# Mixture-of-experts blocks of 32 token slots instead of 64, with four column lanes side by side, in a two-layer backbone on one core

## The reference

```
u = modulate(h, sh2, sc2)
scores = sigmoid(u @ w_router); the best group of 4 experts, in it the best 2
hid = silu(x @ w_gate[e]) * (x @ w_up[e])       # 1024 -> 512, per expert e
y   = hid @ w_down[e]                           # 512 -> 1024
out = sum over the 2 chosen experts of y * score / (sum of the 2 scores)
h = layer_norm(DN_ALPHA * h + g2 * out, ln_g, ln_b)
```

## Time and profile before

| | |
|---|---|
| median of the runs | 1379.34 us |
| profiled execution: time, span | 1381.63 us, 1379.8 us |
| PE busy | 1174.8 us, 85% of the span |
| PE weight loads busy | 663.1 us, 48% |
| DVE, ACT, POOL busy | 543.6, 245.6, 192.9 us |
| mean granted TensorE clock | 0.923 of full |
| gate and up, lines 1307 and 1309, busy on their lanes | 352.0 and 352.6 us |
| down, line 1333 | 186.8 us |
| POOL copy 448, mean; gather 443, mean, median landing | 1.05; 1.12, 6.9 us |
| table loads of line 642 | 25, 1.28 us each |
| DMA traffic | 335.32 MB, mean 243 GB/s |

### The profile page before, as it was taken

One profiled execution on the slowest core, in us unless ns is written; L12 is line 12 of the kernel. 1 busy time (PEld: TensorE's weight loads), 2 busy tenths in 40 slices (PEclk: granted clock), 3 DMA queues, 4 the chain that ended last, 5 costly groups with the idle time before them and its releaser, 6 DMA issues.

```text
span 1379.8 us, 18949 instructions
## 1 busy us (share of the span) xinstructions
PE 1174.8 (85%) x6946; PEld 663.1 (48%) x6947; DVE 543.6 (39%) x1319; ACT 245.6 (18%) x606; POOL 192.9 (14%) x166
## 2 busy tenths in 40 slices
PE   3999799998985999999984399989679999999940
PEld 0444344454453565666542244444445666655620
DVE  0246543462555333333322703036543333333338
ACT  0222333341120111111112111021101111111110
POOL 0011100000001111111111332300021111111123
PEclk9899999998986999999987699999779999999975
DMA  9921399982242999739995782151549996689933
GB/s 326 382 77 61 137 355 352 360 320 100 83 182 69 362 381 374 268 94 368 383 380 178 232 292 89 61 213 46 198 136 382 378 375 213 228 285 373 373 119 135
DMA packets 142758, 335.32 MB, mean 243 GB/s; under 512 B 6872, under 2 KB 9344, under 8 KB 142592
## 3 DMA queue, kind: packets, MB, share of 16 engines
q1 hardware_dynamic: 122400, 286.88, 57.1%
q0 software_dynamic: 6624, 22.55, 5.5%
q10 hardware_dynamic: 13696, 25.38, 5.4%
HBM read 315.40 MB, written 27.79 MB: 249 GB/s over the span
## 4 chain that ended last, share of the span: by engine, by line
PE 75%; DVE 9%; SPq 6%; DMA 5%; issue 2%; ACT 1%; POOL 0%; ACTq 0%; DVEq 0%; PEldq 0%; POOLq 0%
PE PS L1307 13%; PE PS L1333 11%; PE PS L1309 9%; PE PS L1240 8%; PE PS L1391 8%; PE PS L1150 7%; SPq L302 4%; PE PS L1170 3%; PE PS L1086 3%; PE PS L1270 2%; PE PS L1181 2%; DMA ring<-in_e_up_dram 2%; PE PS L1317 2%; DMA RD<-expert_rows,yidx 2%; PE PS L1275 2%
## 5 line engine op out<-in xcount | busy, mean ns | idle before, releaser
L1307 PE MATMUL PS<-ring,RE 128*64 128x256 f32 x1120 | 257.1, 389 | 22.8 <-DVE RE L973 10.3
L1309 PE MATMUL PS<-ring,RE 128*64 128x256 f32 x1120 | 257.5, 390 | 0.0
L1307 PEld LDWEIGHTS PS<-ring,RE 128*64 128x64 f32 x1120 | 155.7, 141 | 81.6 <-issue 46.0
L1001 DVE TENSOR_TENSOR RE<-RE,PS 64x256 f32<-64x256 f32 x100 | 42.3, 423 | 352.9 <-ACT RE L647 352.9
L1309 PEld LDWEIGHTS PS<-ring,RE 128*64 128x64 f32 x1120 | 155.6, 141 | 28.5 <-issue 7.0
L1333 PE MATMUL PS<-ring,RE 128*64 128x512 f32 x560 | 136.2, 602 | 0.0
L1240 PE MATMUL PS<-ring,uT 128*128 128x512 f32 x256 | 111.2, 593 | 1.9 <-ACT G L611 1.1
L1391 PE MATMUL PS<-ring,uT 128*128 128x512 f32 x256 | 110.0, 592 | 0.0
L448 POOL COPY RFW<-RE 64x1024 f32<-64x1024 f32 x50 | 52.3, 1046 | 404.4 <-PE PS L1275 390.1
L1307 PE MATMUL PS<-uT,RE 128*64 128x256 f32 x416 | 94.9, 387 | 5.0 <-DMA RD<-in_e_up_dram 4.1
L1309 PE MATMUL PS<-RD,RE 128*64 128x256 f32 x416 | 95.1, 388 | 0.0
(11 more groups left out here) (214 smaller groups left out, 1482.4 us busy)
## 6 DMA issues: line engine op xcount, KB each, us to landing
ring<-in_w_ada_dram SPq DMA_DIRECT2D x24, 2048.0 KB, 12.0
ring<-in_e_gate_dram SPq DMA_DIRECT2D x22, 2048.0 KB, 16.3
ring<-in_e_up_dram SPq DMA_DIRECT2D x22, 2048.0 KB, 19.0
ring<-in_e_down_dram SPq DMA_DIRECT2D x22, 2048.0 KB, 20.0
RD<-in_e_up_dram SPq DMA_DIRECT2D x10, 2048.0 KB, 22.8
RFW<-in_e_down_dram SPq DMA_DIRECT2D x10, 2048.0 KB, 21.7
uT<-in_e_gate_dram SPq DMA_DIRECT2D x10, 2048.0 KB, 17.1
ring<-in_b_win_dram SPq DMA_DIRECT2D x4, 2048.0 KB, 8.3
```

The lines of the kernel that those rows point to most:

```text
L1001: V_.tensor_tensor(hid[:, 256 * h:256 * h + 256], gs[:, 256 * h:256 * h + 256], PS[BLK:P, h, 0:256], ALU.mult).then_inc(hid_rd[l][h], 1)
L1307: mm(PS[0:BLK, h, 0:256], xT[:, k, :], wg[:, k, 256 * h:256 * h + 256], start=(k == 0), stop=(k == DC - 1))
L1309: ins = mm(PS[BLK:P, h, 0:256], xT[:, k, :], wu[:, k, 256 * h:256 * h + 256], start=(k == 0), stop=(k == DC - 1))
```

## The change

`BLK` becomes 32, and `CG` = 128 / 32 = 4 is the number of column lanes. Gate and up each split in two halves of 256 columns, so that four matmuls of 256 columns (gate 0, gate 1, up 0, up 1) share one moment and one PSUM bank at partitions 0, 32, 64 and 96. Down splits the 1024 output columns in four lanes of 256. The silu and the product work on 64 partitions (both gate halves below each other) in two pieces of 128 columns, both behind the whole of gate and up, and one transpose of such a piece turns two hidden chunks at once. A block's output is 128 x 256 and goes out in four stores of 32 rows x 1 KB.

The row numbers of all blocks are made at once ahead of the loop: a slot number is split in its low five bits and the rest, and eight matmuls of two one-hot factors give a table `gidx` of 32 x 52. POOL has two gather buffers and copies the column that a gather reads to `gcol`. The Silu activation that makes the table load stands ahead of ACT's loop.

```diff
-BLK = 64
+BLK = 32
+CG = P // BLK
@@ row numbers, DVE
-                link(V_.tensor_copy(srel[:, :, :], slot[:, :, :]))
+                link(V_.tensor_scalar(sli[:, :, :], yidx[:, :, :], BLK - 1, None, ALU.bitwise_and))
+                link(V_.tensor_copy(slo[:, :, :], sli[:, :, :]))
+                link(V_.tensor_tensor(shi[:, :, :], slot[:, :, :], slo[:, :, :], ALU.subtract))
+                V_.tensor_tensor(ohlo, slo[:, :, :].rearrange("p k t -> p (k t)").unsqueeze(2).broadcast_to([P, 2 * NT, BLK]),
+                                 iota_s.unsqueeze(1).broadcast_to([P, 2 * NT, BLK]), ALU.is_equal)
+                for k in range(2):
+                    for j in range(NT):
+                        ins = V_.tensor_scalar(ohhi[:, NT * k + j, :], iota_b, shi[:, k, j:j + 1], tokid[:, j:j + 1],
+                                               ALU.is_equal, ALU.mult)
+                ins.then_inc(oh_rd[l], 1)
+                dve.wait_ge(ix_pe[l], 1)
+                V_.tensor_copy(gidx[:, :], PS[0:BLK, 6, 0:NCOL]).then_inc(ix_rd[l], 1)
@@ GpSimd, in the loop
-                        pool.wait_ge(xg_in[l], g * 16 + 16)
+                        pool.wait_ge(xg_in[l][1 - par], gg * 16 + 16)
+                        nc.gpsimd.tensor_copy(gcol[:, 1 - par:2 - par], gidx[:, bass.ds(g + 3, 1)]).then_inc(gc_used[l], 1)
                         pool.wait_ge(xt_pe[l], g + 1)
-                        hand_over()
-                        pool.wait_ge(ix_rd[l], g + 3)
+                        nc.gpsimd.tensor_copy(xg, xga[1 - par]).then_inc(xg_rd[l], 1)
...
-                        gather(par)
+                        gather(xga[1 - par], xg_in[l][1 - par], gcol[:, 1 - par:2 - par])
@@ ScalarE
+                A(warm[:, :], ones[:, 0:1], ACT.Silu)
                 with act.Fori(0, pairs) as gg:
-                    A(warm[:, :], ones[:, 0:1], ACT.Silu)
                     for par in range(2):
                         g = gg * 2 + par
+                        act.wait_ge(gu[l], g + 1)
                         for h in range(2):
-                            act.wait_ge(gu[l][h], g + 1)
-                            A(gs[:, 256 * h:256 * h + 256], PS[0:BLK, h, 0:256], ACT.Silu).then_inc(silu_rd[l][h], 1)
+                            A(gs[:, P * h:P * h + P], PS[0:2 * BLK, 0, P * h:P * h + P], ACT.Silu).then_inc(silu_rd[l][h], 1)
+                        for h in range(2):
                             act.wait_ge(ht_pe[l][h], g + 1)
-                            A(hidT[:, 2 * h:2 * h + 2, :], PS[:, 3 + h, 0:2 * BLK].rearrange("p (k s) -> p k s", k=2),
+                            A(hidT[:, h, :, :], PS[:, 3 + h, 0:2 * BLK].rearrange("p (h s) -> p h s", h=2),
                               ACT.Copy).then_inc(ht_rd[l][h], 1)
                         act.wait_ge(y_ev[l], g + 1)
-                        for q in range(2):
-                            act.dma_start(yscr[l][bass.ds(g * BLK, BLK), 512 * q:512 * q + 512],
+                        for q in range(CG):
+                            act.dma_start(yscr[l][bass.ds(g * BLK, BLK), 256 * q:256 * q + 256],
                                           ysb[par][BLK * q:BLK * q + BLK, :]).then_inc(y_st[l][par], 16)
@@ VectorE, in the loop: index(), onehot() and the wait for the gather go; the two products are
+                            V_.tensor_tensor(hid[:, P * h:P * h + P], gs[:, P * h:P * h + P],
+                                             PS[2 * BLK:P, 0, P * h:P * h + P], ALU.mult).then_inc(hid_rd[l][h], 1)
@@ TensorE, ahead of the loop
+                for n in range(2 * NT):
+                    ins = mm(PS[0:BLK, 6, 0:NCOL], ohlo[:, n, :], ohhi[:, n, :], start=(n == 0), stop=(n == 2 * NT - 1))
@@ TensorE, in the loop
+                        for k in range(DC):
+                            for q in range(CG):
+                                w, h = (wg, wu)[q // 2], q % 2
+                                ins = mm(PS[BLK * q:BLK * q + BLK, 0, 0:256], xT[:, k, :], w[:, k, 256 * h:256 * h + 256],
                                          start=(k == 0), stop=(k == DC - 1))
+                        ins.then_inc(gu[l], 1)
                         pe.wait_ge(xg_rd[l], g + 1)
                         turn_x()
+                        for h in range(2):
+                            pe.wait_ge(hid_rd[l][h], g + 1)
+                            nc.tensor.transpose(PS[:, 3 + h, 0:2 * BLK], hid[:, P * h:P * h + P],
+                                                ident[0:2 * BLK, 0:2 * BLK]).then_inc(ht_pe[l][h], 1)
                         landed(2)
+                        for h in range(2):
                             pe.wait_ge(ht_rd[l][h], g + 1)
+                            for k in (h, h + 2):
+                                for q in range(CG):
+                                    ins = mm(PS[BLK * q:BLK * q + BLK, 5, 0:256], hidT[:, h, k // 2, :],
+                                             wd[:, k, 256 * q:256 * q + 256], start=(k == 0), stop=(k == FC - 1))
+                        ins.then_inc(dn_pe[l], 1)
```

More of the change, by code:

```diff
@@ L51, in backbone @@
     NTHR = TOK // BLK - 1
+    NCOL = MAXB + 4
     SH1, SC1, G1, SH2, SC2, G2 = range(0, 6 * DC, DC)
@@ L161, in backbone @@
         slot = sb("slot", [P, 2, NT])
-        srel = sb("srel", [P, 2, NT])
+        slo = sb("slo", [P, 2, NT])
+        shi = sb("shi", [P, 2, NT])
+        sli = sb("sli", [P, 2, NT], I32)
         yidx = sb("yidx", [P, 2, NT], I32)
         table = [sb(f"table{l}", [1, NE + 3], I32) for l in range(DEPTH)]
-        gidx = sb("gidx", [P, 2], I32)
+        gidx = sb("gidx", [BLK, NCOL], I32)
+        gcol = sb("gcol", [BLK, 2], I32)
         at = {}
-        for name, width in (("slot", BLK), ("dec16", NE), ("dec4", NG), ("token", NT), ("thr", NTHR), ("pair", MAXB // 2)):
+        for name, width in (("slot", BLK), ("dec16", NE), ("dec4", NG), ("token", NT), ("thr", NTHR), ("pair", MAXB // 2),
+                            ("block", NCOL)):
             first = sum(b - a for a, b in at.values())
             at[name] = (first, first + width)
-        ic = sb("ic", [P, first + width], I32)
+        ic = RE[:, 512:512 + first + width].bitcast(I32)
         fc = sb("fc", [P, first + width])
-        iota_s, dec16, dec4, tokid, thr, even = (fc[:, a:b] for a, b in at.values())
+        iota_s, dec16, dec4, tokid, thr, even, iota_b = (fc[:, a:b] for a, b in at.values())
         PS = st.enter_context(nc.psum_tensor("PS", [P, 8, 512], F32))
@@ L245, in backbone @@
         ix_rd = [sem(f"index_ready_{l}") for l in L]
-        xg_in = [sem(f"gathered_{l}") for l in L]
+        xg_in = [[sem(f"gathered_{l}_{b}") for b in range(2)] for l in L]
         x0_in = [sem(f"block_0_gathered_{l}") for l in L]
@@ L250, in backbone @@
         xT_rd = [sem(f"block_xT_ready_{l}") for l in L]
-        gu = [[sem(f"gate_up_{h}_in_psum_{l}") for h in range(2)] for l in L]
+        gu = [sem(f"gate_up_in_psum_{l}") for l in L]
         silu_rd = [[sem(f"silu_{h}_ready_{l}") for h in range(2)] for l in L]
@@ L258, in backbone @@
         y_st = [[sem(f"block_out_stored_{l}_{b}") for b in range(2)] for l in L]
+        gc_used = [sem(f"gather_column_{l}") for l in L]
         dlp = [sem(f"dve_loop_chain_{l}") for l in L]
@@ L372, in follow @@
                     for j in range(3):
-                        sp.wait_ge(dn_pe[l] if j == 2 else gu[l][1], last)
+                        sp.wait_ge(dn_pe[l] if j == 2 else gu[l], last)
                         sp.nop(nofuse=True)
@@ L411, in _ @@
             iota("thr", BLK, BLK, 0)
-            iota("pair", 2, 0, 0).then_inc(s_ic, 1)
+            iota("pair", 2, 0, 0)
+            iota("block", BLK, 0, 0).then_inc(s_ic, 1)
             pool.wait_ge(s_rope, 32)
@@ L974, in x_evac @@
                                      ALU.add).then_inc(xT_rd[l], 1)
-                onehot(link)
-                for b in range(3):
-                    if b == 2:
-                        dve.wait_ge(x0_in[l], 16)
-                    dve.wait_ge(ix_pe[l], b + 1)
-                    index(b % 2)
-                    onehot(link)
                 affine(l, NT - 2)
@@ L994, in lnk @@
                         ins.then_inc(loop, 1)
-                        dve.wait_ge(loop, gg * 6 + k[0])
+                        dve.wait_ge(loop, gg * 2 + k[0])
                     for par in range(2):
@@ L1265, in moe @@
                 mm(PS[:, 5, 64:80], ones[:, :], MP[:, NT, :], start=True, stop=True).then_inc(rk_pe, 1)
-                def index():
-                    for j in range(NT):
-                        ins = mm(PS[0:BLK, 6, 0:1], oh[:, j, :], tokid[:, j:j + 1], start=(j == 0), stop=(j == NT - 1))
-                    ins.then_inc(ix_pe[l], 1)
+                pe.wait_ge(oh_rd[l], 1)
+                for n in range(2 * NT):
+                    ins = mm(PS[0:BLK, 6, 0:NCOL], ohlo[:, n, :], ohhi[:, n, :], start=(n == 0), stop=(n == 2 * NT - 1))
+                ins.then_inc(ix_pe[l], 1)
                 def turn_x():
@@ L1277, in turn_x @@
```

(5 more changed lines are left out.)

113 lines of the change are left out of this document (35 added, 78 removed).

## The result

The changed kernel takes 1367.12 us (median of 4 runs, 1365.63 to 1368.86) against 1379.62 us for the kernel before on the same chip (4 runs): ratio 0.9907, 95% interval 0.989 to 0.9924. It is faster by 12.5 us, 0.9%. The forecast was 1369.5.

The account below looks back on a forecast made before the run. TensorE was taken to set most of the time, with expert-weight loads close behind. Layer 0 +1.1, layer 1 -4.8 and tail -6.1 sum to -9.8 us, giving 1369.5 us; range 1346 to 1411, the forecast's own 1348 to 1382.

Parts of the forecast that it names:

- Four lanes are four wide: Gate and up: four column lanes run as two do, so 16 steps take 3.47 us.
- Rivals A and B: Gate/up lanes: A, a third lost, 1461 to 1492 us, chance 0.11; B, only two at once, near 1728, chance 0.08.
- The block: One block of 32 within an expert, down to down: 6.95 us, bounds 6.7 and 7.25.
- ScalarE's stores: Issuing four stores per block takes 2.42 us, hidden before the next silu with 0.0 to 0.2 us to spare.
- C: Rival: the block's open chain or ScalarE's stores are longer than forecast, block 7.25 to 7.7 us; chance 0.23.
- Changes of expert: PE's table reads between experts cost 1.04 us per change, 1.57 where the outer loop turns; 18.3 us per layer.
- The loads: Expert-weight DMA: 6.05 us per load, ends 5.7 and 6.3; waits 13.6 us in layer 0, 9.6 in layer 1.
- slow starts: An expert's start after a gap over 2 us costs 2.0 us more; 6 us booked in each layer.
- the ledger: Tally of both expert stages from block times, changes, serial weight loads and slow starts: layer 0 +1.1 us, layer 1 -4.8.
- Starts: Both layers' expert loops start 1.9 us earlier, partly because layer norm runs beside the gather.
- Tail: Behind layer 1's last block, PE's end to first gather of results falls from 12.1 to 6.1 us: -6.1.
- Layer by layer: Ends of the expert stages against the kernel before: layer 0 +1.1 us, layer 1 -4.8 us.

Follow-up runs that it names:

- run 2: Changed kernel with gate and up running two column lanes at a time instead of four: 1527.65 us, ratio 1.1065 to the kernel before.
- run 1: Changed kernel with ScalarE's dummy activation that loads the function table back inside its block loop: 1388.44 us, ratio 1.0054 to the kernel before.
- run 7: Changed kernel with each block's rows going out in eight stores of 128 columns instead of four of 256: 1463.66 us, ratio 1.0576.
- runs 5 and 6: Each expert-weight load halved, result no longer the reference's: changed kernel 1332.37 us, ratio 0.9632; kernel before 1370.77 us, ratio 0.9923.
- run 3: Kernel before, blocks of 64 and two lanes kept, with all gather indices made ahead of the loop: 1380.43 us, ratio 1.0002.
- run 8: Changed kernel with gate and up in two column phases, stores one block late, hidden-row transposes spread among the passes: 1386.17 us, ratio 1.0029.
- run 4: Changed kernel with gate and up in two phases of 128 columns and a silu behind each: 1363.87 us, ratio 0.9897.

## Why the prediction was right, point by point

- **Four lanes are four wide.** Right: 64 passes in 3.49 us (predicted 3.47). Rivals A and B are out, by this row and by run 2. They could have been out from the start. I wrote that four lanes had not been seen, but the kernel before has them elsewhere: line 1086 puts matmuls of 512 columns side by side at partitions 0, 32, 64 and 96.

```profile
166.55 1.92 PE L1086 MATMUL PS<-ring,silu_c 128*32 128x512 f32 x16 [0.52 <-DVE mod L730]
```

  That is 16 passes in 1.92 us, where two lanes of the same width take a step of 0.43 us for two passes (down's 8 in 1.77). The "128 in 4.8 us" that I gave for PE's queue I can't find again either: the densest 128 loads and passes of that trace start within 6.6 us, and the densest 16 within 0.35.
- **The block.** 6.95 predicted, 6.83 measured, inside 6.7 to 7.25. The open chain is silu 0.28, product 0.30, transpose 0.26, copy 0.23 and the pick-ups between them. From the silu's start to down's it takes 1.39 us (546.74 to 548.13), and I had 5.16 less 3.77, the same 1.39. The 0.12 us lie elsewhere: 0.05 from the first pass to the silu (543.02 to 546.74, 3.72 for 3.77) and 0.07 in down until the next first pass (1.72 for 1.79).
- **ScalarE's stores.** I had 2.42 us for four and 0.0 to 0.2 to spare; they take 1.75, and in undisturbed blocks end about 0.5 us ahead of the silu (544.47 + 1.75 = 546.22, silu 546.74). The price of a store was wrong by over a quarter, on the safe side. But C was close: one table load more (run 1) or four more stores (run 7) bring it on.
- **Changes of expert.** 1.04 and 1.57 predicted, 0.76 and 1.3 to 1.4 measured; the sum 36.6 against 29.6. The run ahead of PE's sequencer was worth more than the 1.0 us I gave it.
- **The loads.** 6.05 us per load predicted. From 633 to 727 us 33.09 MB went through: 15.8 loads, 5.96 each, and a block's gather and stores 0.8 us. Waits for weights: 23 us predicted with slow starts of 12 beside them; 38.2 measured, and 9.1 for slow starts (2.0 each predicted, 1.0 to 2.9 measured). The step is right, its size is too small by 15 us, and it absorbed what the two steps above it had been overpriced: 79 x 0.12 and 7.0, 16 us. This is why a forecast with three terms off by 7 to 15 us came out 2.4 us from the truth. That blocks and loads trade against each other is the ledger's own mechanism, and runs 5 and 6 show it; that they trade so nearly one for one was not in it. With the measured block, changes and load time, and at its own rates (5 us for 0.1 us of a block, 13.5 for 0.35 us of a load), the ledger would have said some 14 us less, near 1356: an estimate, and some 11 us below what was measured. So the closeness of the number is in part luck, and why the ledger lets the loads off too lightly no run followed up.
- **Starts.** 1.9 us earlier predicted for each layer; 2.3 and 3.1 measured. The reason given was only half of it: the first gather does stand later (426.40 for 424.55), but run 3, with the same table and the same layer norm beside the gather and blocks of 64, wins 0.2 us. The rest stands in rows that get shorter with 32 slots: in that run the index matmuls take 1.93 us, the gather 3.94 and the scaling 0.70 and 1.52, in the changed kernel 1.61, 3.13, 0.44 and 1.20.
- **Tail.** 6.1 predicted, 5.2 measured. The first gather of results stands 4.5 us behind PE's end (1318.63 to 1323.11) where I had 6.1 and before had 12.1; of the 7.6 us won there 2.4 are lost behind it, which no run followed up.
- **Layer by layer.** Layer 0 +1.1 predicted and -2.3 measured at its end, layer 1 -4.8 and -5.4.

What I had not seen is where the blocks are won. By the block counts, twelve experts (five and seven) have one block of 32 where they had one of 64, and each wins 12.2 less 6.83, 64 us in all; the others lose 18 together, as one with eight blocks does (eight times 6.83 are 54.6 us, four times 12.2 are 48.8). But an expert brings three loads, 18 us, and one with a single block computes for 7.6. The gain falls just where the weights set the pace. The waits come seldom and are long: seven ahead of gate and up, 34.8 us; as I read it, where a row of small experts has used up the three that were loaded ahead. They stand at the end of layer 0, behind the first five experts of layer 1, and at its end. At most other changes PE pays only its own 0.76 or 1.3 to 1.4. The crowded experts in the middle are the furthest from the loads (585 to 627 us: PE busy 39.10 of 42, DMA share 0.24), and the largest of them lose by narrow blocks.

## What to carry to other kernels

Ask not only how much work a change takes away but in which stretch, and what sets the pace there: a cut in compute that falls on load-bound stretches is handed back as waiting. An edit that measures as next to nothing may be worth something under another bound (here 2.2 us in the stages with full loads and 29.8 with half), and halving the suspected resource in both versions shows it in two runs. Look for the form you want to try elsewhere in the same trace before you call it unseen. When a loop body gets shorter, engines off its path that had room, here ScalarE with its stores and table load, become the next edge. Whatever makes TensorE wait there can also lower its clock, and then the lateness is paid twice.

## What the runs showed of the hardware

- Four column lanes of 32 run side by side at full width: 16 passes of 512 columns in 1.92 us (kernel before, line 1086), 64 of 256 columns in 3.49 us (changed kernel).
- Column lanes of TensorE keep passes of their own: lanes issued later start while earlier lanes still have passes to run (run 2, six passes within 0.25 us where 0.217 brings two).
- A transpose over several lanes between lane passes takes 0.20 us of PE's chain and 0.14 around it (run 8; read from one block's rows).
- Passes of 128 columns in four lanes go at 27 ns for each pair of load and pass (run 4), the same columns per us as passes of 256.
- A store's issue on ScalarE costs 0.44 to 0.50 us whether it carries 256 or 128 columns (run 7).
- Behind waits the passes themselves get slower: granted clock 0.55 and 3.40 us for down's 32 passes behind 2.70 us in which PE was busy for 1.13, where they take 1.93 at full clock (run 7).
